# Attention heads of a hybrid decoder layer: who normalises the probabilities, and when the value product and its gate are signalled

## What is computed

```python
sc = jnp.einsum('bqhd,bkhd->bhqk', q_blk, k) * scale      # q, k: 128 + 64 wide
sc = jnp.where(key_pos <= q_pos, sc, -jnp.inf)
p  = jax.nn.softmax(sc, axis=-1)
o  = jnp.einsum('bhqk,bkhd->bqhd', p, v)                  # v: 128 wide
o_attn = o * jax.nn.silu(z_attn)
```

## Time and profile before

| | us |
|---|---|
| median of three executions | 1011.03 (1007.6 to 1016.79) |
| the profiled execution, its own time | 1012.25 |
| its span in the trace | 1010.4 |
| TensorE busy in the span | 927.2 |
| VectorE, ScalarE, GpSimd busy | 730.7, 422.1, 237.2 |
| mean granted TensorE clock | 0.978 of full |

### The profile page before, as it was taken

One profiled execution on the slowest core, in us unless ns is written; L12 is line 12 of the kernel. 1 busy time (PEld: TensorE's weight loads), 2 busy tenths in 40 slices (PEclk: granted clock), 3 DMA queues, 4 the chain that ended last, 5 costly groups with the idle time before them and its releaser, 6 DMA issues.

```text
span 1010.4 us, 13744 instructions
## 1 busy us (share of the span) xinstructions
PE 927.2 (92%) x4801; PEld 767.3 (76%) x4801; DVE 730.7 (72%) x1212; ACT 422.1 (42%) x663; POOL 237.2 (23%) x125
## 2 busy tenths in 40 slices
PE   3889999999999999999889988988988989999994
PEld 2668878888778878888677877877877778888883
DVE  4869799755777676677376876867868768548958
ACT  2462243434443455343654444444434434323421
POOL 3322122211221212222541412403415000001404
PEclk9899999999999999999999999999999999999998
DMA  9972213211132231333540420421404319643502
GB/s 283 293 259 54 63 42 124 74 52 42 42 104 84 83 103 42 104 98 117 160 126 14 149 92 35 135 83 55 135 27 152 145 41 392 255 156 125 212 29 83
DMA packets 105290, 117.80 MB, mean 117 GB/s; under 512 B 10117, under 2 KB 83942, under 8 KB 105254
## 3 DMA queue, kind: packets, MB, share of 16 engines
q1 hardware_dynamic: 105094, 116.81, 35.0%
q10 hardware_dynamic: 160, 0.52, 0.2%
HBM read 85.59 MB, written 27.79 MB: 112 GB/s over the span
## 4 chain that ended last, share of the span: by engine, by line
PE 75%; DVE 11%; issue 4%; ACT 4%; SPq 3%; DMA 1%; POOL 1%; DVEq 0%; ACTq 0%; POOLq 0%
PE bank L740 16%; PE bank L741 15%; PE bank L742 15%; PE bank L830 14%; PE bank L985 2%; DVE ptl L1700 1%; PE bank L860 1%; PE bank L901 1%; PE bank L970 1%; PE bank L974 1%; PE bank L971 1%; PE bank L973 1%; PE bank L972 1%; DVE small L1681 1%; PE bank L862 1%
## 5 line engine op out<-in xcount | busy, mean ns | idle before, releaser
L643 POOL TENSOR_TENSOR wl<-wraw,wh 128x1024 fp32r<-128x1024 f32 x32 | 79.4, 2481 | 215.8 <-ACT wh L1156 215.8
L740 PE MATMUL bank<-uh,wh 128*128 128x512 f32 x288 | 116.5, 404 | 5.6 <-ACT ost L1172 2.5
L741 PE MATMUL bank<-ul,wh 128*128 128x512 f32 x288 | 114.6, 398 | 0.0
L742 PE MATMUL bank<-uh,wl 128*128 128x512 f32 x288 | 114.5, 397 | 0.0
L830 PE MATMUL bank<-uh,wh 128*128 128x512 f32 x256 | 103.3, 403 | 0.0
L830 PE MATMUL bank<-ul,wh 128*128 128x512 f32 x256 | 100.8, 394 | 0.0
L740 PE MATMUL bank<-owh,mxh 128*128 128x512 f32 x256 | 100.2, 391 | 0.0
L830 PE MATMUL bank<-uh,wl 128*128 128x512 f32 x256 | 100.2, 391 | 0.0
L742 PE MATMUL bank<-owh,mxl 128*128 128x512 f32 x256 | 99.8, 390 | 0.0
L741 PE MATMUL bank<-owl,mxh 128*128 128x512 f32 x256 | 99.8, 390 | 0.0
L1331 ACT ACTIVATE pth<-bank 128x512 fp32r<-128x512 f32 (+1 forms) x96 | 43.6, 489 | 79.4 <-PE bank L985 40.4
(11 more groups left out here) (224 smaller groups left out, 2289.3 us busy)
## 6 DMA issues: line engine op xcount, KB each, us to landing
wraw<-in_w_in SPq DMA_DIRECT2D x33, 512.0 KB, 3.7
owr<-in_w_out SPq DMA_DIRECT2D x32, 512.0 KB, 4.5
wada<-in_w_ada SPq DMA_DIRECT2D x16, 512.0 KB, 6.1
proj_scratch<-ost SPq DMA_DIRECT2D x16, 512.0 KB, 2.8
xin<-in_x SPq DMA_DIRECT2D x8, 512.0 KB, 6.0
cx<-in_w_ada SPq DMA_DIRECT2D x1, 4096.0 KB, 12.9
ssm_scratch<-xd SPq DMA_DIRECT2D x8, 512.0 KB, 3.5
zs<-proj_scratch SPq DMA_DIRECT2D x8, 512.0 KB, 4.5
```

Source lines behind the costliest of these rows:

```text
L643: pool.tensor_tensor(wl[:, p], wraw[:, p], wh[:, p].bitcast(F32), ALU.subtract).then_inc(w_split, 1)
L740: pe.matmul(dst, ah, bh, start=start, stop=False)
L741: pe.matmul(dst, ah, bl, start=False, stop=False)
L742: return pe.matmul(dst, al, bh, start=False, stop=stop)
```

## The change

It has four parts, all in the heads.

1. The multiply of `prob` by the reciprocal moves from VectorE to ScalarE, as a copy with a per-row scale (`normalise` on ScalarE, waiting on a new semaphore `r_ready`). VectorE keeps the reciprocal alone (`inverse_sum`), without the wait on its own result.
2. TensorE signals a new semaphore `pv_half` after the fourth key tile of `values(1)`, and `turned_high(3)` waits for that instead of `pv_ready`.
3. `gate_out(1)` stands behind `turned_low(3)` instead of behind `turned_low(2)`.
4. The exponentials of row tiles 1 and 0 are placed later (1) or after the turned copies (0): `probs(1)` before `turned_high(3)`, `probs(0)` behind `turned_high(2)`, and their reciprocals accordingly.

```diff
@@ values (TensorE)
+                    if g == 1 and t == 3:
+                        mm.then_inc(pv_half, 1)
@@ ScalarE
+            def normalise(i, h):
+
+                act.wait_ge(r_ready, 8 * h + 8 - i)
+                v = prob[:, i % 2, 0:(i + 1) * P]
+                act.activation(v, v, ACT.Copy, scale=small[:, 16 + i % 2:17 + i % 2]).then_inc(p_ready, 1)
+
@@ turned_high
                     if n == 8:
-                        act.wait_ge(pv_ready, 2 * h + 1)
+                        act.wait_ge(pv_half, h + 1)
@@ head (ScalarE)
                 for i in range(7, -1, -1):
-                    if i >= 1:
+                    if i >= 3:
                         probs(i - 1, b, h)
+                    normalise(i, h)
                     if i in units(odd) and not (isinstance(h, int) and h == 0 and i >= 6):
                         hi_unit(i, h, odd)
+                    if i == 3:
+                        probs(1, b, h)
                     turned_high(i, h)
+                    if i == 2:
+                        probs(0, b, h)
@@ VectorE
-            def normalise(i, h):
+            def inverse_sum(i, h):
                 dve.wait_ge(exp_done, 8 * h + 8 - i)
-                ch.link(dve.reciprocal(small[:, 16 + i % 2:17 + i % 2], small[:, 12 + i % 2:13 + i % 2]))
-                n = (i + 1) * P
-                dve.tensor_scalar(prob[:, i % 2, 0:n], prob[:, i % 2, 0:n], small[:, 16 + i % 2:17 + i % 2], None,
-                                  ALU.mult).then_inc(p_ready, 1)
+                dve.reciprocal(small[:, 16 + i % 2:17 + i % 2], small[:, 12 + i % 2:13 + i % 2]).then_inc(r_ready, 1)
@@ head (VectorE)
-                normalise(7, h)
                 for i in range(7, -1, -1):
-                    if i >= 1:
-                        normalise(i - 1, h)
+                    if i >= 3:
+                        inverse_sum(i - 1, h)
                     if i in units(odd) and not (isinstance(h, int) and h == 0 and i >= 6):
                         lo_unit(i, h, odd)
                     if i >= 2:
                         row_max(i - 2, h)
+                    if i == 3:
+                        inverse_sum(1, h)
                     turned_low(i, h)
+                    if i == 3:
+                        gate_out(1, h)
                     if i == 2:
-                        gate_out(1, h)
+                        inverse_sum(0, h)
...
                 row_max(7, h + 1)
                 row_max(6, h + 1)
                 gate_out(0, h)
+                inverse_sum(7, h + 1)
```

More of the change, by code:

```diff
@@ L292, in build_layer @@
         exp_done = sem("exp_done")
+        r_ready = sem("r_ready")
         p_ready = sem("p_ready")
@@ L296, in build_layer @@
         pt_split = sem("pt_split")
+        pv_half = sem("pv_half")
         pv_ready = sem("pv_ready")
@@ L1752, in head @@
                 gate_out(0, h)
+                inverse_sum(7, h + 1)
             def last_head(h):
-                normalise(7, h)
                 for i in range(7, -1, -1):
-                    if i >= 1:
-                        normalise(i - 1, h)
+                    if i >= 3:
+                        inverse_sum(i - 1, h)
                     if i >= 2:
                         row_max(i - 2, h)
+                    if i == 3:
+                        inverse_sum(1, h)
                     turned_low(i, h)
+                    if i == 3:
+                        gate_out(1, h)
+                    if i == 2:
+                        inverse_sum(0, h)
                     if 2 <= i <= 5:
                         out_low(5 - i)
-                    if i == 2:
-                        gate_out(1, h)
                 gate_out(0, h)
@@ L1776, in _ @@
             row_max(6, 0)
+            inverse_sum(7, 0)
             head(0, 0)
-            per = 2 * (8 * 2 + 8)
+            per = 2 * (8 * 2)
             ch.loop(0, per)
```

## The result

The changed kernel takes 998.47 us, median of four executions (996.78 to 1001.55), beside 1009.32 us for the kernel before on the same chip: ratio 0.988, 95% interval 0.9838 to 0.9922, so a gain of about 1.2% that is clear of no change. The profiled execution took 1001.55 us, 10.7 less than the 1012.25 of before, with a span of 999.7. The forecast was 1000.3 for this execution and 999 for the median.

A forecast was written before the change was run, and what follows sets the result against it. TensorE, busy 92% of the span, was taken as the bound, with time won only where it waits or runs slowly. 48.7 us go, 36.8 come: 11.9 less, 1012.25 to 1000.3 profiled, median 999, range 990 to 1008.

The forecast's parts named there:

- The gate product's 21.7 us: TensorE's seven waits at `unit(1)` for VectorE's gate product go: 19.6 us plus 0.3 for each.
- The low-half and multiply waits, 16.8 us: TensorE's eleven waits for low halves of transposed probabilities (15.3 us) and one for the multiply (1.5) go.
- The new waits: TensorE's transposes wait for ScalarE's scaled copy: 3.9 us per even head, 3.5 odd, 7.8 last, 5.1 first; 35.1 in all.
- The scaled copies: 64 copies on ScalarE, 49 us in all; one pointer operand taken to cost 0.09 us over the plain copy.
- The clock: Six half-clock stretches on TensorE behind gate waits, 10.2 us, go; one of 1.7 us is counted behind the new waits.
- VectorE's busy time: A sign in the changed profile: VectorE's busy time 45 to 48 us lower, ScalarE's some 49 higher.
- The clock falling in every head (1011): Rival: TensorE's clock still falls about once per head, eight stretches in place of one, adding 11.9 us: 1011; chance 0.1.
- three or four fall: Smaller case of the clock rival: three or four half-clock stretches, 1004 us; chance 0.2 shared with dear copies.
- The slower end: Rival: ScalarE paces every row tile (7 us more) and TensorE falls to half clock twice per head (24): 1030; chance 0.06.
- The dear copy: Rival: scaled copies cost the full 0.19, 3.5 us, and 4 of 15.3 low-half waits stay: 1006 to 1007; chance 0.2, shared.
- the cheap copy: Rival: no pointer cost (3.3 us less), no clock stretch (1.7), further stalls gone (about 3): 991; chance 0.14.
- The argument that speaks against the change: Multiplies are 33 us of undisturbed work on VectorE, 49 on ScalarE; 16 us would be lost: 1028; chance 0.01.

The follow-up runs named there:

- the first experiment: The changed kernel with the multiply of the probabilities back on VectorE, half signal and early gate product kept: 986.26 us, ratio 0.976 to the kernel before.
- the four pairs in the table: Multiply on VectorE against ScalarE, by gate product and signal place: behind/end 1008.8, 1020.3; behind/fourth tile 1007.0, 1013.9; early/end 991.2, 1004.7; early/fourth tile 986.3, 998.5 us.
- that of 980.3: The changed kernel with the multiply back on VectorE, and there the low half of row tile 4 set ahead of row_max(2): 980.33 us, ratio 0.9698.

## Why the prediction was right, and where not

**The total** was right within 1.3 us: 11.9 predicted for the profiled execution, 10.7 measured. Its main terms, on the prediction's own basis of 0.3 per wait for start to start:

- The gate product's 21.7 us went, as laid out: copy released 1.8 us ahead of the group's end (1.9 predicted), no wait left at `unit(1)`.
- The low-half and multiply waits, 16.8 us, went from TensorE's matmuls, and for the reason given: except in the odd heads VectorE's low halves were in time or nearly so. But it was not pure gain, as the sum had it: the first experiment shows that VectorE can keep the multiply and TensorE waits 13.7 for it, half of what it waits for the scaled copy.
- The new waits: 35.1 predicted. The table has 25.7 in 24 places, with 0.3 each 32.9. An even head has 0.63, 1.12 and 0.77 us in three places, an odd one 1.84 and 0.96, the last 5.99 in five. With 0.3 each, row tile 1 and the odd and last heads are near their terms (2.1 for 2.1 at the odd heads' row tile 4). The small waits predicted at row tiles 6 and 3 of the even heads, 0.7 together, did not come:

```profile
604.19 0.87 PE L987 MATMUL bank<-ident,prob 128*128 128x128 f32 x6 [0.63 <-ACT prob L1330]
...
608.49 0.76 PE L987 MATMUL bank<-ident,prob 128*128 128x128 f32 x5 [1.12 <-ACT prob L1330]
...
646.19 0.76 PE L987 MATMUL bank<-ident,prob 128*128 128x128 f32 x5 [1.84 <-ACT prob L1330]
...
799.43 0.65 PE L987 MATMUL bank<-ident,prob 128*128 128x128 f32 x4 [2.08 <-ACT prob L1330]
```

- The scaled copies were sized right, 1.147, 0.930, 0.825 and 0.496 us against 1.15, 0.93, 0.82 and 0.50. So one pointer operand costs 0.09 us over the plain copy:

```profile
L1330 ACT ACTIVATE prob<-prob,small 128x1024 f32<-128x1024 f32 x8 | 9.2, 1147 | 0.0
...
L1330 ACT ACTIVATE prob<-prob,small 128x512 f32<-128x512 f32 x8 | 5.8, 720 | 0.0
```

- The clock is the term that was mis-sized. The prediction let five of six half-clock stretches go, since "shorter gaps, the eleven of up to 2.2 us, show no such stretch near them". In the trace three are left. Two stand behind odd heads' waits of 1.84 us (0.53 over 647 to 649 above), one behind the last head's wait of 2.08. At 1.7 each, three fewer are 5.1, not 8.5. With these sizes the sum is 38.5 gone, 32.9 come, 5.1 of clock, 10.7, where the stage itself is 10.0 shorter and the execution 10.7. That the total was nearly met is in part luck: the new waits were put 2.2 too high and the clock's gain 3.4 too high, and the two nearly cancelled. The clock also varies by execution: its mean ran from 0.975 to 0.987 over the executions of the kernel before, and the profiled one, from which the six stretches were counted, had 0.978.
- VectorE's busy time fell by 39.5 where 45 to 48 was said, ScalarE's rose by 43.4 where it was 49. The copies do sum to 49.2 us by their rows, but neighbouring rows of an engine overlap, and busy time counts that once:

```profile
603.14 0.92 ACT L1330 ACTIVATE prob<-prob,small 128x768 f32<-128x768 f32 x1
603.97 0.58 ACT L1305 ACTIVATE vh<-bank 128x512 fp32r<-128x512 f32 x1
```

  With 0.09 for each of 64 (an estimate from this one pair) this is 5.8, the whole of ScalarE's difference, and as much of VectorE's; 2.5 us there stay unexplained.

**The rivals.** The clock falling in every head (1011) did not happen, but its mechanism is what was left, in three places. That is the smaller case of this rival, "three or four fall", for which 1004 was named; the time stayed under it because the new waits were shorter than laid out. The slower end, paced by ScalarE and chopped into half clock, was named as a mechanism at 0.06 and did not come in the whole change; alone, the moved multiply does end slower than before, by 0.7%. Its new waits for the copy are there, and half clock only once more than before in the profiled execution; the median clock of its five executions (0.981) is that of the kernel before within 0.002. The dear copy and the cheap copy are out by the durations.

**The argument that speaks against the change** was dismissed too readily. The sum of undisturbed work (33 us on VectorE, 49 on ScalarE) gave 1028 and was given 0.01. As a time it was wrong; as a verdict on this part it was right. What makes the move dear is not the sum of work. The copy stands on the chain from row maximum to transposes, in ScalarE's queue, and TensorE waits 25.7 us for it, while the multiplies on VectorE, stalls included, leave 13.7 us of waits. The Trainium skill, page "ScalarE: Activation LUTs", section "Rules for kernel authors", says that a multiply belongs on VectorE; by that rule the four pairs in the table agree, with 7 to 14 us each.

## What to carry to other kernels

Test the parts of a change apart before keeping the whole: here one line, the gate product's place, was worth more than the whole change, and one part took back half of what the others gave. Place work by which instruction the bottleneck engine waits for next and what stands ahead of it in the queue, not by which engine has idle time. When an instruction is set forward, ask what the one behind it feeds: it paid at row tile 4 and cost at row tile 5.

## What the runs showed of the hardware

- A VectorE multiply from SBUF to SBUF, with a pointer scale, is held by GpSimd's running operation on SBUF: 1416 ns for 512 elements in the mean of eight, 603 with GpSimd's operations cut short, while 768 elements without GpSimd beside them take 620. The Trainium skill, page "GPSIMD Engine Reference", section "1. Specifications", lists GpSimd's SBUF interfaces as shared with VectorE, with contention for VectorE instructions in a two-port performance mode or with two SBUF inputs. The two traces agree that there is contention and add its price; no run shows which of the two cases this multiply is. ScalarE's scaled copy was not held: twenty of its 64 instances ran beside an operation of GpSimd, and none took over 0.03 us more than the others of its size (the longest of all 1.155 us, beside a mean of 1.147 for 1024 elements).
- Half clock does not only follow the 2.4 us waits. It was at 0.50 behind one of 1.85 us and at 1.00 behind one of 1.64, in the same place of the same head:

```profile
642.00:644.00 2.00, 2.00 (x7) 1.61 (x6) 2.00 (x2) 0.77 (x2) 2.00 (x2) 0.50 0.00 0
```
```profile
641.00:643.00 2.00, 2.00 (x12) 1.57 (x10) 2.00 (x2) 0.75 (x2) 2.00 (x2) 1.00 0.00 0
```

  The first is the version of 986.3 us, the second that of 980.3. In the changed kernel, waits of 1.84 us had it behind them in two odd heads and not in the first, and one of 1.86 in the last head had none. The kernel with the row maximum first has waits of 1.83 and 2.09 us in the same places and no half clock in the heads. So a length alone does not decide it.
- Busy time of the same matmuls ran from 267.7 to 281.9 us over these kernels, and mostly followed the idle time. Seven half-clock stretches in the slowest, at 1.7 us each, against none in the fastest make 11.9 of the 14.2. So a wait taken out gave back more than its length here.
- The same kernel's executions differ with the granted clock. Of twelve with the signal alone, the four fastest (1002.4 to 1006.3 us) had a mean clock of 0.986 to 0.990, the five slowest (1008.07 to 1010.4) 0.978 to 0.980. Of twelve with the signal and the new places, the four fastest (1002.3 to 1004.3) had 0.987, the four slowest (1009.2 to 1011.6) 0.980 to 0.982. Every execution of the kernel before above 1014.9 us whose clock was measured had 0.980 or less. The waits of 2.3 us do not bring this scatter by themselves: the changed kernel with the gate product behind has them too, and its ten executions lie within 3.1 us (0.979 to 0.985).
